# One expert block moved from behind a retrieval head to behind the last scores, and the weight split moved inside GpSimd's decoding

## The chip, the cores and the metric

The kernel runs on one core of one Trainium2 chip. The metric is the time of one execution on the device, in microseconds (us), lower is better. Its engines are TensorE (PE; its weight loads are PEld), VectorE (DVE), ScalarE (ACT), GpSimd (POOL) and the queue of SyncE (SP), which issues most DMAs.

## What is computed

One layer of a decoder with 1024 tokens of width 1024: a first half that mixes tokens, then a PEER layer: eight heads each pick 16 of 128 x 128 experts by product keys. The change touches the retrieval of this second half and the products with expert rows that are made ahead beside it.

```python
q = (hf @ w_query).reshape(n, PEER_HEADS, 2, PEER_HALF)
scores = jnp.einsum('nhpd,hpkd->nhpk', q, sub_keys).astype(jnp.float32)
s_top, i_top = lax.top_k(scores, PEER_TOPK)
cand_s = (s_top[:, :, 0, :, None] + s_top[:, :, 1, None, :]).reshape(n, PEER_HEADS, PEER_TOPK * PEER_TOPK)
cand_i = (i_top[:, :, 0, :, None] * N_KEYS + i_top[:, :, 1, None, :]).reshape(n, PEER_HEADS, PEER_TOPK * PEER_TOPK)
best_s, best_pos = lax.top_k(cand_s, PEER_TOPK)
idx = jnp.take_along_axis(cand_i, best_pos, axis=-1)
gates = jax.nn.softmax(best_s, axis=-1).astype(h.dtype)
...
u = jnp.take(expert_u, idx_blk, axis=0)
act = jax.nn.gelu(jnp.einsum('thkd,td->thk', u, h_blk))
```

## The kernel before

Products in float32 are made as three passes over upper and lower halves: an operand is split into an upper part (`hi`) and the rest (`lo`). The function `retrieve` is one block of programs, one for each engine; they meet only at its end and are otherwise ordered by semaphores and by the order of each program.

**Heads.** For each head d of 8, TensorE makes four units of queries (L195, 24 matmuls of 128x512 each) and two groups of scores (L1511) with the keys. ScalarE copies queries (L1581) and scores (L1590) out of the banks. VectorE searches the scores for the best 16 of either half (`search`, L1643 to L1655), adds them and ranks the sums (`combine`, L1672 on; it raises `ranked`). GpSimd then decodes the places (`decode`, L1459 to L1477), subtracts them from a row of numbers (L1482), ScalarE makes one-hots of the difference (`one_hot`, L1575 and L1577), GpSimd multiplies these by the indices (L1488), and VectorE sums them up (`conclude`, L1713, L1715, L1718), for head h - 1 behind the ranking of head h. ScalarE also takes the exponentials of a ranked head (`exponentials`, L1564 and L1567), at the beginning of the chunk two heads later.

**Query weights** come in a ring of two slots. SP loads one (L159) when the slot's raw part has been split, ScalarE makes the upper half (`split_hi`, L164), GpSimd the lower half (`split_lo`, L170, 128x2048). TensorE starts head d when both are there. In GpSimd's program the split for head h + 2 stands ahead of `decode(h)`, so that of head h + 3 stands directly behind the multiplications of head h.

**Blocks ahead.** Beside the heads TensorE already makes products with blocks of 128 expert rows (class `Ahead`), which the dense part of the expert stage reads later. A block n is: `turn` (L1343, eight transposes of the rows loaded by L1328), ScalarE's `upper` copy (L1369), `leave` (L1351, TensorE subtracts the upper part in the bank), ScalarE's `lower` copy (L1376), `hide` (L1361, two times 24 matmuls of 128x320), ScalarE's `gelu` (L1383) of either half, and SP's `store` (L1332). `turn` waits for both GELUs of the block before. There are 21 blocks: nine in `retrieve`, twelve in the scatter stage behind it. Of the nine, six stand in heads 2 to 7 (`IN_HEADS`, `FIRST` = 2), three behind the last scores (`IN_TAIL`).

**Tail.** Behind the last scores each of the three blocks also has two halves of rows (`rows_by_token`, L1544) that TensorE turns back to rows of tokens and ScalarE copies to `h_rows` (L1629), six halves in all. ScalarE has `exponentials(6)` ahead of the tail's blocks, `one_hot(6)` in the first of them ahead of its GELUs, and `exponentials(7)` in the last ahead of its GELUs. VectorE searches and ranks head 7 meanwhile, decodes it itself, concludes heads 6 and 7 and normalises the gates; the last step waits for `exponentials(7)`. SP waits at the end for the last store to land.

Of the kernel before, what the change touches and what calls it, by code (L numbers as in the profile page):

```python
# [37 lines left out]
PH, TOPK, NKEYS = 8, 16, 128  # L38
# [258 lines left out]
class Middle:  # L297


    U = 8  # L300
# [985 lines left out]
class Ahead:  # L1286


    FIRST, IN_HEADS, IN_TAIL = 2, 6, 3
    HEADS = IN_HEADS + IN_TAIL  # L1290
    EVERY = NKEYS // 8
    EXTRA = 5
# [101 lines left out]
def retrieve(nc, core, t, ring, begin, w_query, h, pick_i, pick_j, gate, ahead, h_rows):  # L1394
# [26 lines left out]
    last_ab, last_iota = core.at("rt_last_ab", 82, [P, 2, HB, 2], BF16), core.at("rt_last_iota", 83, [P, TOPK, 2], BF16)  # L1421
    last_place, last_eighth, last_less = (core.at(f"rt_last_part{k}", 84 + k / 2, [P, TT * TOPK]) for k in range(3))
    h_turned, h_copied = (core.sem(f"rt_{n}", lasting=RETRIEVE) for n in ("h_turned", "h_copied"))
    NPAIR, U = PH // 2, 4
    JOBS, FIRST_JOB = ahead.IN_HEADS, ahead.FIRST

    with nc.Block() as block:

        @block.sync
        def _(sp):  # L1430
            def query_weights(d):
                ring.load(sp, d % 2, d // 2, [(0, w_query[0, :, d * CW:(d + 1) * CW])])

            query_weights(2)
            query_weights(3)
            ahead.load(sp, 0, 0)
            ahead.load(sp, 1, 1)
            query_weights(4)
            query_weights(5)
            for n in range(ahead.HEADS):  # L1440
                if n + 2 < ahead.HEADS:
                    ahead.load(sp, n + 2, n % 2)
                for half in range(2):
                    ahead.store(sp, n, half)
                if n + 6 < PH:
                    query_weights(n + 6)
            for half in range(2):
                sp.wait_ge(ahead.stored[half], ahead.HEADS * 16)

        @block.gpsimd  # L1450
        def _(pool):
            pool.sem_inc(ring.lo_done[1], 1)
            ring.split_lo(nc.gpsimd, pool, 1, 0, U)

            def decode(h, s):

                pl, (a, b) = place[:].rearrange("p t k -> p (t k)"), (ab[s][:, 0, :], ab[s][:, 1, :])
                pool.wait_ge(ranked, h + 1)
                nc.gpsimd.tensor_copy(place_f[:], pl)  # L1459
                nc.gpsimd.tensor_copy(top_f[s][:], top_i[s])  # L1460
                pool.drain().then_inc(placed, 1)
                nc.gpsimd.tensor_scalar(eighth[:], place_f[:], 0.125, -0.4375, ALU.mult, ALU.add)
                nc.gpsimd.tensor_scalar(less[:], place_f[:], float(TOPK), 8.0, ALU.is_lt, ALU.mult)
                pool.drain()
                nc.gpsimd.tensor_scalar(eighth[:], eighth[:], ROUND, -ROUND, ALU.add, ALU.add)
                nc.gpsimd.tensor_tensor(less[:], less[:], place_f[:], ALU.add)
                pool.drain()
                nc.gpsimd.tensor_scalar(eighth[:], eighth[:], -1.0, 0.0, ALU.add, ALU.max)
                nc.gpsimd.tensor_scalar(place_f[:], place_f[:], -72.0, 0.0, ALU.add, ALU.max)
                pool.drain()  # L1470
                nc.gpsimd.tensor_tensor(a, place_f[:], eighth[:], ALU.add)
                pool.drain()
                nc.gpsimd.tensor_scalar(place_f[:], a, -8.0, -8.0, ALU.mult, ALU.add)
                pool.drain()
                nc.gpsimd.tensor_tensor(b, place_f[:], less[:], ALU.add)
                pool.drain()
                nc.gpsimd.tensor_scalar(b, b, 0.0, None, ALU.max)  # L1477
                pool.drain()
                if h >= 1:
                    pool.wait_ge(concluded, h)  # L1480
                for p in range(2):
                    nc.gpsimd.tensor_tensor(hot[p], ab[s][:, p, :].unsqueeze(2).to_broadcast([P, TT * TOPK, TOPK]),  # L1482
                                            t.iota16[:].unsqueeze(1).to_broadcast([P, TT * TOPK, TOPK]),
                                            ALU.subtract).then_inc(apart, 1)
                for p in range(2):
                    hot4 = hot[p].rearrange("p (t k) a -> p t k a", t=TT)
                    pool.wait_ge(hot_done, h * 2 + (p + 1))
                    nc.gpsimd.tensor_tensor(hot4, hot4, top_f[s][:, :, p, :].unsqueeze(2).to_broadcast([P, TT, TOPK, TOPK]),  # L1488
                                            ALU.mult).then_inc(picked, 1)

            for i in range(NPAIR - 1):
                for s in range(2):
                    ring.split_lo(nc.gpsimd, pool, s, i + 1, i * 2 * U + (s + 2) * U)
                    decode(i * 2 + s, s)
            decode(PH - 2, 0)
            core.clear_early(pool)

        @block.tensor
        def _(pe):
            ahead.prime_tensor(pe)  # L1500

            def units(d, half, j):
                ring.channels_unit(nc, pe, core.bank[j % 2], d % 2, j % 2, h, half, d * U + j)

            def scores(h, half):
                pe.wait_ge(q_copied, h * U + 2 * half + 2)
                for m in range(2 * half, 2 * half + 2):
                    pe.wait_ge(sc_copied, 4 + h * U + m - 1)
                    for k in range(4):
                        tt, p = 2 * m + k // 2, k % 2  # L1510
                        last = nc.tensor.matmul(core.bank[4 + m % 2][:, k * P:(k + 1) * P], q[:, p, tt * P:(tt + 1) * P],  # L1511
                                                sk_t[:, 2 * h + p, :], start=True, stop=True)
                    last.then_inc(scored, 1)

            for d in range(PH):
                n = d - FIRST_JOB
                job = 0 <= n < JOBS
                if d:
                    ring.ready(pe, d % 2, d // 2)
                    units(d, 0, 0)  # L1520
                if job:
                    ahead.turn(pe, n, n % 2, n // 2)
                if d:
                    units(d, 0, 1)
                scores(d, 0)
                if job:
                    ahead.leave(pe, n, n % 2)
                units(d, 1, 2)
                if job:
                    ahead.hide(pe, n, n % 2, 0)  # L1530
                units(d, 1, 3)
                if job:
                    ahead.hide(pe, n, n % 2, 1)
                scores(d, 1)
            def rows_by_token(n):

                tile, k0 = DENSE // P + n // 2, (n % 2) * 4
                if n < 2:
                    pe.wait_ge(sc_copied, 4 * PH + n + 3)
                else:  # L1540
                    pe.wait_ge(h_copied, n - 1)
                for k in range(4):
                    for a, part in enumerate((h.lo, h.hi)):
                        last = nc.tensor.matmul(core.bank[4 + n % 2][:, k * P:(k + 1) * P],  # L1544
                                                part[:, k0 + k, tile * P:(tile + 1) * P].bitcast(F32), t.ident[:], start=a == 0, stop=a == 1)
                last.then_inc(h_turned, 1)

            for k in range(ahead.IN_TAIL):
                n = JOBS + k
                ahead.turn(pe, n, n % 2, n // 2)  # L1550
                rows_by_token(2 * k)
                ahead.leave(pe, n, n % 2)
                rows_by_token(2 * k + 1)
                for half in range(2):
                    ahead.hide(pe, n, n % 2, half)

        @block.scalar
        def _(act):
# [12 lines left out]
            def one_hot(h):  # L1571

                for p in range(2):
                    act.wait_ge(apart, h * 2 + (p + 1))
                    nc.scalar.activation(hot[p], hot[p], ACT.Square)  # L1575
                    act.drain()
                    nc.scalar.activation(hot[p], hot[p], ACT.Relu, scale=-1.0, bias=1.0).then_inc(hot_done, 1)  # L1577
# [45 lines left out]
            for k in range(ahead.IN_TAIL):  # L1623
                job = JOBS + k
                ahead.upper(act, job, job % 2)
                ahead.lower(act, job, job % 2)
                for n in range(2 * k, 2 * k + 2):
                    act.wait_ge(h_turned, n + 1)
                    nc.scalar.activation(h_rows[:, n // 2, (n % 2) * HALF:(n % 2 + 1) * HALF], core.bank[4 + n % 2], ACT.Copy).then_inc(h_copied, 1)  # L1629
                if k == 0:  # L1630
                    one_hot(PH - 2)
                if k == ahead.IN_TAIL - 1:
                    exponentials(PH - 1)
                for half in range(2):
                    ahead.gelu(act, job, half)
# [1035 lines left out]
```

## Time and profile before

| | |
|---|---|
| runs | 3179.38, 3179.74, 3186.13 us; median 3179.74 |
| profiled execution | 3184.67 us, its span 3182.9 us |
| mean granted clock of TensorE | 0.983 of 2.4 GHz |
| busy share of the span | PE 95%, DVE 77%, POOL 38%, ACT 35% |
| retrieval | 846 to 1151 us of the span |
| scatter stage behind it | 1151 to about 1347 us |
| expert stage | from about 1347 us to the end |

A line of a timeline has the start and the duration of an instruction, or of several merged (x8), its engine, line, operation and operands, and in brackets the idle time of the engine before it and what ended that. Merged rows of matmuls overlap at their ends by some tenths of a microsecond, so the start of the next row tells better when a group was done.

### The profile page before, as it was taken

How to read it: one execution, taken by the hardware profiler on the slowest of the kernel's cores; microseconds unless marked ns; L12 is line 12 of the kernel's file. 1: busy time of each engine (PE TensorE's matmuls, PEld its weight loads, DVE VectorE, ACT ScalarE, POOL GpSimd, SP SyncE). 2: the span in 40 equal slices, each digit the busy share in tenths (PEclk: the TensorE clock that was granted, in tenths of full speed). 3: DMA queues.
4: the chain of work that ended last, by engine and by line, in shares of the span. 5: the costliest groups of instructions: out<-in, count | busy, mean ns of one | idle time of the engine just before them, and what ended most of it. 6: DMA issues, size and time to landing. Idle time of an engine off the chain costs nothing.

```text
span 3182.9 us, 52635 instructions
## 1 busy us (share of the span) xinstructions
PE 3032.1 (95%) x18287; PEld 2699.4 (85%) x18287; DVE 2456.8 (77%) x4956; ACT 1107.2 (35%) x2044; POOL 1206.6 (38%) x966
## 2 busy tenths in 40 slices
PE   6999999999999989969999999999999999999995
PEld 4998888779888878868898898889889888888884
DVE  5455333465589989978888888988888898999987
ACT  4222666503355655522232222222222222222222
POOL 0001000010158710035545545555555555555551
PEclk9999999999999999979999999999999999999998
DMA  6436333234211128899889889988988899999995
GB/s 239 147 123 195 108 107 106 84 119 140 95 37 56 33 74 251 264 349 329 315 319 336 323 311 328 326 300 326 336 325 317 319 334 329 346 339 347 335 333 208
DMA packets 353546, 764.41 MB, mean 240 GB/s; under 512 B 21020, under 2 KB 178808, under 8 KB 353408
## 3 DMA queue, kind: packets, MB, share of 16 engines
q0 software_dynamic: 115712, 419.48, 36.2%
q1 hardware_dynamic: 236640, 338.93, 31.5%
q10 hardware_dynamic: 1056, 4.19, 0.3%
q8 instruction: 82, 1.34, 0.2%
q14 instruction: 56, 0.46, 0.0%
HBM read 688.49 MB, written 74.03 MB: 240 GB/s over the span
## 4 chain that ended last, share of the span: by engine, by line
PE 50%; DVE 5%; issue 3%; DMA 3%; DVEq 2%; ACT 1%; POOL 0%; POOLq 0%; ACTq 0%; SPq 0%
PE psum L2174 22%; PE psum L2181 21%; PE psum L1361 3%; PE psum L2166 2%; PE psum L1876 2%; DVE ex_u_row L2381 2%; DMA ex_un<-in_expert_u 1%; DVE acc L2394 1%; DMA ex_v_row<-in_expert_v,ex_row 1%; DVEq L2391 1%; DVEq L2384 1%; DVE acc L2434 0%; DVE h_lo L2371 0%; PE psum L1343 0%; DVE fi_xs L2566 0%
## 5 line engine op out<-in xcount | busy, mean ns | idle before, releaser
L2122 POOL DMA_INDIRECT ex_u_row<-in_expert_u,ex_row x384 | 446.8, 1164 | 858.2 <-DVE ex_dot L2381 565.4
L2122 POOL DMA_INDIRECT ex_v_row<-in_expert_v,ex_row x384 | 518.4, 1350 | 150.5 <-issue 110.7
L2394 DVE SCALAR_TENSOR_TENSOR acc<-ex_v_row,ex_coef,acc 128x1024 f32<-128x1024 f32 x384 | 492.9, 1284 | 45.0 <-DMA ex_v_row<-in_expert_v,ex_row 17.9
L2381 DVE CUSTOM_DVE_ANT_0 ex_u_row<-ex_u_row,h_rows 128x1024 f32<-128x1024 f32 x384 | 467.3, 1217 | 1.9 <-DMA ex_u_row<-in_expert_u,ex_row 1.6
L2181 PE MATMUL psum<-ex_v_hi,ex_c_lo 128*128 128x512 f32 x1260 | 359.9, 408 | 22.7 <-DVE h_lo L2371 14.2
L2181 PE MATMUL psum<-ex_v_lo,ex_c_hi 128*128 128x512 f32 x1260 | 339.2, 391 | 0.0
L2181 PE MATMUL psum<-ex_v_hi,ex_c_hi 128*128 128x512 f32 x1260 | 338.6, 391 | 0.0
L2174 PE MATMUL psum<-h_hi,h_lo 128*128 128x320 f32 x1712 | 288.2, 311 | 19.2 <-DVE h_lo L2371 19.2
L2174 PE MATMUL psum<-h_lo,h_hi 128*128 128x320 f32 x1712 | 288.3, 311 | 0.0
L2174 PE MATMUL psum<-h_hi 128*128 128x320 f32 x1712 | 286.4, 310 | 0.0
L2174 PEld LDWEIGHTS psum<-h_hi,h_lo 128*128 128x128 f32 x1712 | 263.8, 189 | 24.8 <-DVE h_lo L2371 15.6
L2181 PEld LDWEIGHTS psum<-ex_v_lo,ex_c_hi 128*128 128x128 f32 x1260 | 237.1, 188 | 51.4
L2181 PEld LDWEIGHTS psum<-ex_v_hi,ex_c_hi 128*128 128x128 f32 x1260 | 237.0, 188 | 51.2
L2181 PEld LDWEIGHTS psum<-ex_v_hi,ex_c_lo 128*128 128x128 f32 x1260 | 222.2, 189 | 64.5 <-DVE h_lo L2371 20.1
L2174 PEld LDWEIGHTS psum<-h_lo,h_hi 128*128 128x128 f32 x1712 | 262.3, 189 | 0.0
L2174 PEld LDWEIGHTS psum<-h_hi 128*128 128x128 f32 x1712 | 260.4, 188 | 0.0
L2263 ACT ACTIVATE h_hi<-psum 128x512 fp32r<-128x512 f32 x214 | 127.1, 597 | 311.7 <-PE psum L2166 311.4
L2289 ACT ACTIVATE ex_c_hi<-ex_g 128x320 fp32r<-128x320 f32 x190 | 86.2, 470 | 410.3 <-DVE ex_g L2414 250.2
L2269 ACT ACTIVATE ex_v_hi<-ex_vn 128x2048 fp32r<-128x2048 f32 x63 | 120.2, 1909 | 262.7 <-PE psum L2181 262.7
L2376 DVE TENSOR_TENSOR ex_v_lo<-ex_vn,ex_v_hi 128x2048 fp32r<-128x2048 f32 x63 | 144.4, 2293 | 44.2 <-ACT ex_v_hi L2269 43.9
L2434 DVE TENSOR_TENSOR acc<-psum,acc 128x512 f32<-128x512 f32 x189 | 129.4, 685 | 59.1 <-PE psum L2181 59.1
L2371 DVE TENSOR_TENSOR h_lo<-psum,h_hi 128x512 fp32r<-128x512 f32 x214 | 142.8, 685 | 14.0 <-ACT h_hi L2263 11.6
(347 smaller groups left out, 5447.7 us busy)
## 6 DMA issues: line engine op xcount, KB each, us to landing
ex_vn<-in_expert_v SPq DMA_DIRECT2D x64, 1024.0 KB, 6.3
ex_un<-in_expert_u SPq DMA_DIRECT2D x43, 1024.0 KB, 8.7
w_dram<-sc_w SPq DMA_DIRECT2D x10, 4096.0 KB, 15.0
ex_w<-w_dram SPq DMA_DIRECT2D x64, 640.0 KB, 9.5
gm_wm<-in_w_mod SPq DMA_DIRECT2D x16, 1024.0 KB, 5.1
pj_raw<-in_w_in SPq DMA_DIRECT2D x11, 1024.0 KB, 8.4
ex_un<-in_expert_u SPq DMA_DIRECT2D x21, 512.0 KB, 7.0
qk_dram<-pj_staged_r POOLq DMA_DIRECT2D x32, 256.0 KB, 3.1
```

What stands on the lines that cost most here:

```text
L1361: last = self.nc.tensor.matmul(self.hide_bank[half][:, 0:HD], lhsT, rhs, start=i == 0, stop=i == len(ops) - 1)
L2122: nc.gpsimd.indirect_dma_start(to[:], None, all_rows, bass.IndirectOffsetOnAxis(row[s][:, col:col + 1], 0)).then_inc(done, 16)
L2174: last = nc.tensor.matmul(core.bank[bank][:, 0:HD], lhsT, rhs, start=m == 0, stop=m == len(ops) - 1)
L2181: last = nc.tensor.matmul(out, lhsT, rhs, start=m == 0 and not kept, stop=m == len(ops) - 1, skip_group_check=kept)
L2263: nc.scalar.activation(ut(h.hi, q // 2, (q % 2) * 4, 4), core.bank[banks[q]].rearrange("p (k n) -> p k n", k=4), ACT.Copy).then_inc(u_hi, 1)
L2269: nc.scalar.activation(vh.hi[:], vn[:], ACT.Copy).then_inc(v_hi, 1)
L2289: nc.scalar.activation(c_hi_at[c_set(j)][e][:, half * HD:(half + 1) * HD], x(j, n, first)[:], ACT.Copy).then_inc(c_hi, 1)
L2371: nc.vector.tensor_tensor(ut(h.lo, q // 2, (q % 2) * 4, 4), core.bank[bank].rearrange("p (k n) -> p k n", k=4), ut(h.hi, q // 2, (q % 2) * ...
L2376: nc.vector.tensor_tensor(vh.lo[:], vn[:], vh.hi[:].bitcast(F32), ALU.subtract).then_inc(v_lo, 1)
L2381: nc.vector.tensor_tensor_reduce(out=u_row[k % 3][:], in0=u_row[k % 3][:], in1=h_rows[:, k % 3, :], scale=1.0, scalar=0.0, op0=ALU.mult, o ...
L2394: nc.vector.scalar_tensor_tensor(out=to, in0=v_row[k % 3][:], scalar=coef[:, k:k + 1], in1=to, op0=ALU.mult, op1=ALU.add).then_inc(row_use ...
L2434: nc.vector.tensor_tensor(to, core.bank[banks[n]], to, ALU.add).then_inc(added, 1)
```

## The change

`IN_HEADS` goes from 6 to 5 and `IN_TAIL` from 3 to 4. The five blocks stand in heads 2 to 6, head 7 has none, and four stand behind the last scores. The first of these has no halves of rows beside it; the other three have two each, so that the six halves stand where three blocks are again. `one_hot(6)` stays in the first block of the tail, `exponentials(7)` in the last.

In GpSimd's program the split for head 2 stays ahead of `decode(0)`. Those for heads 3 to 7 go into `decode(h)`, between the subtraction and the multiplications, each with the same waits as before.

```diff
-    FIRST, IN_HEADS, IN_TAIL = 2, 6, 3
+    FIRST, IN_HEADS, IN_TAIL = 2, 5, 4
...
@@ retrieve, decode on GpSimd
                                             ALU.subtract).then_inc(apart, 1)
+                if h + 3 < PH:
+                    ring.split_lo(nc.gpsimd, pool, (h + 3) % 2, (h + 3) // 2, (h + 3) * U)
                 for p in range(2):
                     hot4 = hot[p].rearrange("p (t k) a -> p t k a", t=TT)
                     pool.wait_ge(hot_done, h * 2 + (p + 1))
...
-            for i in range(NPAIR - 1):
-                for s in range(2):
-                    ring.split_lo(nc.gpsimd, pool, s, i + 1, i * 2 * U + (s + 2) * U)
-                    decode(i * 2 + s, s)
-            decode(PH - 2, 0)
+            ring.split_lo(nc.gpsimd, pool, 0, 1, 2 * U)
+            for d in range(PH - 1):
+                decode(d, d % 2)
...
@@ retrieve, tail on TensorE
                 ahead.turn(pe, n, n % 2, n // 2)
-                rows_by_token(2 * k)
+                if k:
+                    rows_by_token(2 * k - 2)
                 ahead.leave(pe, n, n % 2)
-                rows_by_token(2 * k + 1)
+                if k:
+                    rows_by_token(2 * k - 1)
...
@@ retrieve, tail on ScalarE
-                for n in range(2 * k, 2 * k + 2):
+                for n in range(2 * max(k, 1) - 2, 2 * k):
```

## Rows read from the trace of the kernel before

**Rows 1.** Windows: length; busy of PE, PEld, DVE, ACT, POOL; clock; DMA share; GB/s.

```profile
967.00:1002.00 35.00, 34.29 (x188) 29.95 (x188) 33.92 (x202) 21.95 (x40) 27.45 (x19) 1.00 0.17 59
...
1122.00:1126.00 4.00, 3.82 (x22) 3.85 (x23) 3.71 (x26) 1.21 (x3) 2.48 (x1) 0.63 0.23 86
1126.00:1136.00 10.00, 9.95 (x70) 9.61 (x69) 9.28 (x56) 2.62 (x6) 0.00 (x0) 0.98 0.04 16
...
1160.00:1164.00 4.00, 3.39 (x12) 2.35 (x13) 4.00 (x4) 1.79 (x3) 0.00 (x0) 0.50 0.41 121
```

**Rows 2.** Timeline of TensorE, scores: heads 0 and 1, 6 and 7.

```profile
863.95 2.05 PE L1511 MATMUL psum<-rt_sk_t,rt_q 128*128 128x128 f32 x16 [0.71 <-ACTq L1582]
...
891.32 2.05 PE L1511 MATMUL psum<-rt_sk_t,rt_q 128*128 128x128 f32 x16 [0.71 <-ACTq L1582]
...
1044.91 2.05 PE L1511 MATMUL psum<-rt_sk_t,rt_q 128*128 128x128 f32 x16 [0.71 <-ACTq L1582]
...
1079.67 2.05 PE L1511 MATMUL psum<-rt_sk_t,rt_q 128*128 128x128 f32 x16 [0.71 <-ACTq L1582]
...
1099.97 1.94 PE L1511 MATMUL psum<-rt_sk_t,rt_q 128*128 128x128 f32 x16
```

**Rows 3.** Timeline of GpSimd, heads 4 to 6.

```profile
1052.43 8.23 POOL L1488 TENSOR_TENSOR rt_hots<-rt_hots,rt_top_f 128x2048 bf16<-128x2048 bf16 x2 [6.02 <-ACT rt_hots L1577]
1060.61 4.65 POOL L170 TENSOR_TENSOR rt_w_lo<-rt_raw,rt_w_hi 128x2048 fp32r<-128x2048 f32 x1
...
1097.31 0.29 POOL L1459 CAST rt_part<-rt_place 128x128 f32<-128x128 uint32 x1 [1.86 <-DVEq L1684]
...
1105.60 7.32 POOL L1482 TENSOR_TENSOR rt_hots<-rt_ab,iota 128x2048 bf16<-128x2048 f32 x2
```

**Rows 4.** Timeline of VectorE: conclusions, searches, the last step.

```profile
922.98 4.34 DVE L1713 TENSOR_TENSOR rt_hots<-rt_hots 128x2048 bf16<-128x2048 bf16 x1
...
1062.58 3.77 DVE L1713 TENSOR_TENSOR rt_hots<-rt_hots 128x2048 bf16<-128x2048 bf16 x1
...
1068.61 0.29 DVE L1643 MAX8 rt_top<-rt_sc 128x8 f32<-128x128 f32 x1
...
1097.32 1.35 DVE L1713 TENSOR_TENSOR rt_hots<-rt_hots 128x2048 bf16<-128x2048 bf16 x1
...
1102.60 0.28 DVE L1643 MAX8 rt_top<-rt_sc 128x8 f32<-128x128 f32 x1 [1.76 <-issue]
...
1146.81 1.23 DVE L1753 TENSOR_TENSOR pick<-pick,rt_einv 128x1024 f32<-128x1024 f32 x1
```

**Rows 5.** Line L1713: durations in ns (least, median, most), first and last start.

```profile
L1713 DVE TENSOR_TENSOR rt_hots<-rt_hots x7: 1226/3661/4342, 923.0 to 1139.0; 128x2048 bf16<-128x2048 bf16 x7
```

**Rows 6.** Timeline of ScalarE: scores of head 6, then the tail.

```profile
1067.20 0.60 ACT L1590 ACTIVATE rt_sc<-psum 128x512 f32<-128x512 f32 x1 [0.30 <-PE psum L1511]
...
1104.51 0.22 ACT L1564 ACTIVATE rt_lowest<-rt_best 128x8 f32<-128x8 f32 x1
1104.79 1.28 ACT L1567 ACT_TABLE_LOAD   x1
...
1108.43 1.05 ACT L1369 ACTIVATE ah_hi<-psum 128x512 fp32r<-128x512 f32 x2
...
1112.34 1.90 ACT L1575 ACTIVATE rt_hots<-rt_hots 128x2048 bf16<-128x2048 bf16 x1
...
1118.10 1.91 ACT L1577 ACTIVATE rt_hots<-rt_hots 128x2048 bf16<-128x2048 bf16 x1
```

**Rows 7.** Timeline of TensorE: second and third block of the tail, next stage.

```profile
1122.18 1.16 PE L1343 MATMUL psum<-ident,ah_un_rt 128*128 128x128 f32 x8 [3.34 <-issue]
...
1136.53 1.06 PE L1343 MATMUL psum<-ident,ah_un_rt 128*128 128x128 f32 x8 [0.57 <-issue]
...
1147.33 1.33 PE L1361 MATMUL psum<-h_hi,ah_hi 128*128 128x320 f32 x8
1151.43 2.81 PE L1815 MATMUL psum<-ident,pick 128*128 128x128 f32 x24 [2.76 <-PEq L1427]
```

More of the change, by code:

```diff
@@ L1423, in retrieve @@
     h_turned, h_copied = (core.sem(f"rt_{n}", lasting=RETRIEVE) for n in ("h_turned", "h_copied"))
-    NPAIR, U = PH // 2, 4
+    U = 4
     JOBS, FIRST_JOB = ahead.IN_HEADS, ahead.FIRST
```

## The prediction

> **What bounds the kernel now.** The edit lies in one stage, the retrieval (846 to 1151 us of the span), so I leave the shares of the whole run and read that stage engine by engine, in the timeline. In its heads the reader is to look for the engine that is never idle. It is TensorE: a head with a block ahead takes 34.76 us, and in every such head TensorE waits once, 0.71 us, for ScalarE's copy of the queries [rows 1, 2]. GpSimd waits 6.0 us in each head for ScalarE's one-hot passes [rows 3]. VectorE looks full in the same window [rows 1], but part of that is no work: its first halving of the one-hots (L1713) takes 1.23 us where GpSimd is still. In the five heads in which it starts while GpSimd runs the weight split of L170 it takes 3.64 to 4.34 us, and ends about 1.2 us after that split [rows 3 to 5]. So VectorE has at least 2.4 us of slack in a head, and in the last head it shows in the open: with no split beside it L1713 takes 1.35 us, and then VectorE waits 1.76 us for scores [rows 4].
>
> Behind the last scores there are two chains. VectorE searches the last head and ends at 1148.0 (1146.81 + 1.23) [rows 4]. TensorE does three blocks and six halves of rows, ends at 1148.66, and what follows it (the GELU, its store, the landing, the meeting of all engines) opens the next stage at 1151.43 [rows 7]. TensorE's chain is the later one, by 0.6 us of its own and 2.8 us of what follows. This tail is not dense: a block can turn only when ScalarE has written the GELUs of the block before, and for the second of the three that came behind the one-hot passes of head 6, with TensorE idle for 3.34 us.
>
> **The split of query weights (first edit).** Nothing is added or removed; five splits of 4.63 us (heads 3 to 7) go from behind GpSimd's multiplications to ahead of them. Their slot is GpSimd's 6.0 us wait: the subtraction ends at 1046.4, the split would end at 1051.1, and the multiplication may start at 1052.4 [rows 3]. Cost 0. If that cover were gone, up to 4.6 us per head would lie between the one-hot passes and VectorE's halving. The loads of later weights are issued sooner on SP's queue; nobody waits for them now. VectorE's halving then meets only GpSimd's short casts, so the row with 1.35 us is the one to take, and the five stretched ones, some 2.5 us each, give back about 12.4 us. What is late next is the scores, and they come from TensorE: in the present run search 6 starts at 1068.61 and its scores were copied at 1067.80 [rows 4, 6]. So VectorE can gain 0.76 us before it waits again, and the rest of the 12.4 us becomes waiting.
>
> The Trainium skill, page "SBUF — State Buffer", section "Who interferes with whom", says that a VectorE instruction with two SBUF inputs and a GpSimd instruction that reads SBUF exclude each other, and that VectorE instructions with one SBUF input, as its searches are, go untouched. The trace agrees on both. Read by that rule alone the edit would be worth 12.4 us; read by the idle time ahead of the searches it is worth 0.76 us.
>
> **Five blocks in the heads (second edit), head 7.** Its block goes. From the second scores of head 0 to those of head 1, which has no block and two waits of 0.71 us, are 27.37 us; with a block a head takes 7.39 more [rows 2]. The last scores end at 1094.4, not 1101.8. What is that worth? VectorE can take them only when it has finished head 6: search 6 starts at 1067.85, its ranking ends 0.76 us earlier than now, at 1096.5, and conclusion 5 ends at 1100.1. So search 7 starts 2.5 us earlier than 1102.60. VectorE's chain gains 2.5 us, and it was not the later one.
>
> **The tail, four blocks.** First block (number 5), from 1094.4. ScalarE's program has head 6's exponentials, which need its ranking, ahead of its copies, so ScalarE stands until 1096.5. Before, this ranking was 7 us old when ScalarE got there (1104.51) [rows 6]. Exponentials take 2.6 us (3.92 less a table load of 1.28, which in the rows follows a GELU; if it stays, it hides in the next wait), then come upper and lower copies, and TensorE's products run from 1102 to about 1109. No rows stand beside the waits of this block: they are moved to the blocks behind it. Then ScalarE's order is one-hot, GELU. GpSimd starts to decode head 6 at 1096.55, takes 8.29 us to the subtraction and 3.67 us for its first half: 1108.5 [rows 3]. The two one-hots take 7.67 us, to 1116.2; from their end to the next turn are 2.17 us, for a table load and the GELUs [rows 6, 7]. The second block turns at 1118.4, against 1122.18 now: only 3.7 us earlier, though the last scores are 7.4 us earlier; TensorE idles about 9 us before it.
>
> From there go three blocks with two halves of rows each, where there are two now. The one behind the gap takes 14.35 us from turn to turn (1122.18 to 1136.53); its first 4 us ran at a mean granted clock of 0.63 (mostly 1.2 GHz), for which it pays about 1.6 us [rows 1, 7]. The next takes 12.13 us to the end of its products and 0.58 for GELU and handover, 12.71; the last 12.13. Sum: 1118.44 + 14.35 + 12.71 + 12.13 = 1157.63, against 1148.66: **+9.0 us.** The last exponentials stand beside the last products as now; VectorE normalises until about 1157, ahead of the store. The later stages start at the same meeting and hold the same twelve blocks, so they are shifted whole: 0.
>
> Against the profiled execution (3184.67 us, its span 3182.9) this is 3193.7. That execution is 4.9 us above the median; on the median, 3179.7 + 9.0 = **3188.7 us**. What no row shows is the clock behind 9 us of idling instead of 3.3. From below, the block pays nothing for it, -1.6 us; from above, the 4 us run at 0.50, as those behind the 6.3 us gap ahead of the next stage did, +0.4 [rows 1]. I take the present price, of the nearest kind of work. With 1 us either way for handovers, and 2 us above because no gap in the rows is so long: 3186.1 to 3192.1 for this case.
>
> **Rivals.** *VectorE sets the pace of the heads.* Then all of the 12.4 us is real: head 6's ranking comes at 1084.9 instead of 1097.3, the 63.9 us from it to the next stage stay, and that opens at 1148.8: -2.6 us, 3177.1. It decides if TensorE waits for VectorE anywhere in the heads. For it: VectorE is busy 97% of the window in rows 1; the skill's rule above is its mechanism. Against: TensorE has one wait per head, on ScalarE's copy. 7%. *GpSimd sets the pace*: five heads shorter by 4.63 us, ranking at 1074.1: -13.4 us, 3166.3. Against stand its own 6 us of waiting. 4%.
>
> *The first block of the tail is not held by the one-hots.* If its GELU came right behind its products, the second turn would come at 1109.8, and the same 39.2 us from there end at 1149.0, against 1148.66: +0.3, 3180.0, no change. Against: the order of ScalarE's program, and the present run's turn at 1122.18, directly behind the GELUs. 7%.
>
> *The clock stays low.* If TensorE runs the whole second block at 1.2 GHz, its remaining 9.5 us double: +18.5, 3198.2. For it: behind both gaps in rows 1 the clock was low; against: 4 us later its mean was 0.98 [rows 1]. 8%. The skill's page "TensorE: Matmul & The Clock Gate", section "HAM oscillation", warns of idle gaps between stretches of matmuls; the second edit makes such a gap longer. By the trace a gap costs 1.6 us, and the present run has it too.
>
> **How the numbers follow.** My case has 74%. A measurement of this kernel can tell about 0.2%, 6.4 us, from no change; the lower end of my case and the scatter of the runs (3179.38 to 3186.13) reach it: 0.62 slower, 0.12 same. With the rivals: slower 0.70; same 0.12 + 0.05 + 0.07 = 0.24; faster 0.04 + 0.02 = 0.06. The range takes in my case, the rival without change and the one with the low clock: 3178.5 to 3198.5; the two of the pace, and an odd run, are left out.
>
> **What would show it.** Heads 2 to 6 keep 34.76 us, L1713 falls to about 1.35 us, and the searches wait for scores about 2 us per head. GpSimd's wait at L1488 falls by about 1 us only, since it starts decoding sooner. The last scores end near 1094.4. TensorE then has two gaps, about 5 us ahead of the first subtraction and about 9 us ahead of the second turn (near 1118), and ends near 1157.6; the next stage opens near 1160.4. I am wrong if the heads shorten, if the second turn comes before 1112, or if a later stage gives the 9 us back.

## The result

| | us | ratio to before |
|---|---|---|
| before, first measurement | 3180.68 median of 5 runs (3179.38 to 3187.54) | |
| changed | 3196.23 median of 5 runs (3189.01 to 3197.46) | 1.0033, 95% interval 1.0022 to 1.0043 |
| profiled execution of the changed kernel | 3195.86, its span 3194.1 | |

The change makes the kernel slower by 0.33% (10.5 us of 3183). The difference of the two medians, 15.5 us, says more than it should: five runs of a kernel spread over 8 us, and in 28 runs beside the experiments the kernel before had a median of 3184.44. The ratio with its interval is what counts.

For the traces a measure is wanted that doesn't depend on how the earlier stages fell. The retrieval of the changed kernel's profile began 2.8 us earlier than that of before (its first scores of head 6 are at 1042.08, before at 1044.91 [rows 2]). The same shift already stands at the second scores of head 0 (861.11 against 863.95 [rows 2]), ahead of everything that the edits touch, so the change can't have caused it. So all times of the tail are counted here from these first scores of head 6. From there the next stage opened after 106.52 us before (1151.43 - 1044.91) and after 116.10 us now: **+9.6 us**.

The heads. Timeline of TensorE, scores of the changed kernel, beside [rows 2]:

```profile
1007.32 2.05 PE L1511 MATMUL psum<-rt_sk_t,rt_q 128*128 128x128 f32 x16 [0.71 <-ACTq L1584]
...
1042.08 2.05 PE L1511 MATMUL psum<-rt_sk_t,rt_q 128*128 128x128 f32 x16 [0.71 <-ACTq L1584]
...
1075.95 2.05 PE L1511 MATMUL psum<-rt_sk_t,rt_q 128*128 128x128 f32 x16 [0.71 <-ACTq L1584]
...
1089.63 2.05 PE L1511 MATMUL psum<-rt_sk_t,rt_q 128*128 128x128 f32 x16 [0.71 <-ACTq L1584]
```

From 1007.32 to 1042.08 are 34.76 us, as before. The last scores begin 47.55 us after the first of head 6, before 55.06 (1099.97 - 1044.91), and the wait of 0.71 us now stands ahead of them.

The moved split. Timeline of GpSimd (the split, then the multiplications of head 4), then of VectorE, conclusion and search of head 6, beside [rows 3, 4]:

```profile
1039.92 4.56 POOL L170 TENSOR_TENSOR rt_w_lo<-rt_raw,rt_w_hi 128x2048 fp32r<-128x2048 f32 x1
1049.61 8.25 POOL L1490 TENSOR_TENSOR rt_hots<-rt_hots,rt_top_f 128x2048 bf16<-128x2048 bf16 x2 [5.12 <-ACT rt_hots L1579]
1058.94 0.29 POOL L1459 CAST rt_part<-rt_place 128x128 f32<-128x128 uint32 x1 [1.09 <-DVEq L1686]
```

```profile
1058.96 1.35 DVE L1715 TENSOR_TENSOR rt_hots<-rt_hots 128x2048 bf16<-128x2048 bf16 x1
1065.02 0.28 DVE L1645 MAX8 rt_top<-rt_sc 128x8 f32<-128x128 f32 x1 [2.54 <-issue]
```

The split is done 5.1 us before GpSimd may go on, the halving (now L1715) takes 1.35 us, and VectorE then waits 2.54 us for scores that it did not have to wait for before (2.30 to 2.55 us in the five heads that had a stretched halving).

The tail. Timeline of TensorE, first products and the turns of the second to fourth block, the last products and the next stage, beside [rows 7]:

```profile
1096.93 1.27 PE L1351 MATMUL psum<-ah_hi,minus 128*128 128x512 f32 x2 [4.37 <-ACT ah_hi L1369]
...
1115.57 1.94 PE L1343 MATMUL psum<-ident,ah_un_rt 128*128 128x128 f32 x8 [7.40 <-issue]
...
1130.56 1.07 PE L1343 MATMUL psum<-ident,ah_un_rt 128*128 128x128 f32 x8 [0.57 <-issue]
...
1143.28 1.06 PE L1343 MATMUL psum<-ident,ah_un_rt 128*128 128x128 f32 x8 [0.57 <-issue]
...
1154.08 1.34 PE L1361 MATMUL psum<-h_hi,ah_hi 128*128 128x320 f32 x8
1158.18 4.32 PE L1817 MATMUL psum<-ident,pick 128*128 128x128 f32 x24 [2.76 <-PEq L1427]
```

TensorE waits 4.37 us for ScalarE's upper copy and 7.40 us ahead of the second turn. ScalarE at the same time, beside [rows 6]: it waits for the ranking, then for GpSimd's subtraction (its one-hots are now L1577 and L1579).

```profile
1093.67 0.21 ACT L1566 ACTIVATE rt_lowest<-rt_best 128x8 f32<-128x8 f32 x1 [1.35 <-DVEq L1686]
...
1105.72 1.91 ACT L1577 ACTIVATE rt_hots<-rt_hots 128x2048 bf16<-128x2048 bf16 x1 [6.87 <-POOL rt_hots L1482]
...
1111.48 1.91 ACT L1579 ACTIVATE rt_hots<-rt_hots 128x2048 bf16<-128x2048 bf16 x1
1113.41 1.28 ACT L1383 ACT_TABLE_LOAD   x1
1114.70 0.77 ACT L1383 ACTIVATE ah_g_rt<-psum 128x320 f32<-128x320 f32 x2
```

The GELUs end at 1115.47 (1114.70 + 0.77), the turn begins at 1115.57. VectorE is not the later chain; its last step waited 12.6 us for `exponentials(7)`:

```profile
1152.93 0.55 DVE L1752 RECIPROCAL rt_einv<-rt_esum 128x64 f32<-128x64 f32 x1 [12.60 <-ACT pick L1569]
```

### The profile page after: what moved, and what is told of

It reads as the page before. It is cut to its first block, busy times and chain, and to the rows that moved or that the text cites. A ratio compares the mean times of both kernels' runs of the same rounds, so it can differ in the third digit from the quotient of the medians.

```text
span 3194.1 us, 52633 instructions
## 1 busy us (share of the span) xinstructions
PE 3034.0 (95%) x18287; PEld 2699.4 (85%) x18287; DVE 2444.5 (77%) x4956; ACT 1105.1 (35%) x2042; POOL 1203.2 (38%) x966
## 4 chain that ended last, share of the span: by engine, by line
PE 50%; DVE 5%; issue 3%; DMA 2%; DVEq 2%; ACT 1%; POOL 0%; POOLq 0%; ACTq 0%; SPq 0%
PE psum L2176 22%; PE psum L2183 21%; PE psum L1361 3%; PE psum L2168 2%; PE psum L1878 2%; DVE ex_u_row L2383 2%; DMA ex_un<-in_expert_u 1%; DVE acc L2396 1%; DVEq L2393 1%; DMA ex_v_row<-in_expert_v,ex_row 1%; DVEq L2386 1%; DVE acc L2436 0%; DVE h_lo L2373 0%; PE psum L1343 0%; DVE fi_xs L2568 0%
## 6 DMA issues: line engine op xcount, KB each, us to landing
w_dram<-sc_w SPq DMA_DIRECT2D x10, 4096.0 KB, 14.9
```

## The experiments

Each is timed against the kernel before on the same chip. The table puts them side by side; the times of the tail are counted from the first scores of head 6, "first turn" is that of the next stage. The traces are of one execution each. Nine lie within 2 us of the median of their kernel; that of e8_three is the fastest of its 11 runs (3178.15 us, median 3184.17), so its trace may flatter it.

| kernel | second turn | next stage opens | first turn there | ratio to before (95%) |
|---|---|---|---|---|
| before | 77.3 | 106.5 | 115.6 | 1 |
| changed | 73.5 | 116.1 | 126.7 | 1.0033 (1.0022 to 1.0043) |
| e1_blocks_only | 74.3 | 117.4 | 128.2 | 1.0031 (1.0018 to 1.0043) |
| e2_split_only | 77.3 | 106.5 | 116.7 | 1.0000 (0.9991 to 1.0009) |
| e3_onehot_later | 66.5 | 109.7 | 118.9 | 1.0013 (1.0004 to 1.0022) |
| e4_rows_first | 73.5 | 114.2 | 123.4 | 1.0026 (1.0015 to 1.0036) |
| e5_both | 65.2 | 107.7 | 118.2 | 1.0006 (0.9997 to 1.0015) |
| e6_before_onehot_later | 74.5 | 108.4 | 119.2 | 1.0013 (1.0004 to 1.0023) |
| e7_exp_later | 73.5 | 116.0 | 126.4 | 1.0033 (1.0021 to 1.0046) |
| e8_three | 62.1 | 101.9 | 112.5 | 0.9996 (0.9987 to 1.0005) |

### The two edits apart

**e1_blocks_only**: five and four blocks, the split where it was before.

```diff
-                if h + 3 < PH:
-                    ring.split_lo(nc.gpsimd, pool, (h + 3) % 2, (h + 3) // 2, (h + 3) * U)
...
-            ring.split_lo(nc.gpsimd, pool, 0, 1, 2 * U)
-            for d in range(PH - 1):
-                decode(d, d % 2)
+            for i in range(NPAIR - 1):
+                for s in range(2):
+                    ring.split_lo(nc.gpsimd, pool, s, i + 1, i * 2 * U + (s + 2) * U)
+                    decode(i * 2 + s, s)
+            decode(PH - 2, 0)
```

> The block is moved, the split stays behind GpSimd's multiplications. Measure: from the first scores of head 6 to the opening of the next stage, 106.5 us in the kernel before, 116.1 in the changed one. My theory (the whole loss is the tail's): 116.9, since only the 0.8 us that head 6's ranking gained are given back; L1713 again 3.6 to 4.3 us in five heads; ratio to before 1.003. Rival (the split inside the decoding costs a part of the loss): 113 or less.

Measured: 117.4 us and 1.0031. The whole loss is there without the split's move. The halvings are stretched again:

```profile
L1715 DVE TENSOR_TENSOR rt_hots<-rt_hots x7: 1225/3664/4365, 921.3 to 1135.7; 128x2048 bf16<-128x2048 bf16 x7
```

Of the 1.3 us more than in the changed kernel, 0.8 are in the second turn (74.3 against 73.5), as the later ranking had to give; the other 0.5 are in the block behind it, 15.5 against 15.0 us from turn to turn.

**e2_split_only**: the kernel before with the split inside the decoding, the same lines the other way round.

> The split is moved, the blocks stay six and three. My theory (TensorE sets the pace of the heads): the heads keep 34.76 us, L1713 falls to about 1.35 us, the searches wait about 2 us more per head, and from the first scores of head 6 to the next stage are 106.5 us as before; ratio 1.000. Rival (VectorE sets the pace): five heads shorter by about 2.5 us, 12 us faster, ratio 0.996. Second rival (the split is not covered by the wait): heads longer by up to 4.6 us.

Measured: 106.5 us and 1.0000. Timeline of VectorE, head 6:

```profile
1061.86 1.35 DVE L1713 TENSOR_TENSOR rt_hots<-rt_hots 128x2048 bf16<-128x2048 bf16 x1
...
1067.92 0.28 DVE L1643 MAX8 rt_top<-rt_sc 128x8 f32<-128x128 f32 x1 [2.53 <-issue]
```

Five halvings gave back some 2.4 us each, and VectorE waits 2.53 us instead: the rival in which VectorE sets the pace is gone (it wanted 0.996). The split inside the decoding costs nothing either.

### What holds the second turn

**e3_onehot_later**: the changed kernel, head 6's one-hots in the second block of the tail.

```diff
-                if k == 0:
+                if k == 1:
                     one_hot(PH - 2)
```

> The changed kernel with head 6's one-hots one block later in ScalarE's tail. My theory (the second turn is held by these one-hots): it comes about 8 us earlier, directly behind the first block's products, the third turn about 15 us after it, and from the first scores of head 6 to the next stage are 107.6 us instead of 116.1; ratio to before about 1.0005. Rival (the loss is the fourth block's own work on TensorE, or the clock): 116, ratio 1.003.

Measured: 109.7 us, 1.0013. The second turn comes 7.0 us earlier, 0.57 us behind the first block's products:

```profile
1111.23 1.07 PE L1343 MATMUL psum<-ident,ah_un_rt 128*128 128x128 f32 x8 [0.57 <-issue]
...
1125.28 1.25 PE L1343 MATMUL psum<-ident,ah_un_rt 128*128 128x128 f32 x8 [1.91 <-issue]
...
1139.62 1.06 PE L1343 MATMUL psum<-ident,ah_un_rt 128*128 128x128 f32 x8 [0.57 <-issue]
```

So the hold was the one-hots: 6.4 of the 9.6 us go with it, though TensorE has the same work. Of the 2.1 us by which I missed, the second turn has 1.5 (at 66.5, where my sum had 65; under the first products, from 1098 to 1106, the granted clock was 0.59 and then 0.56) and the third block 1.6 (14.34 us against 12.7 for one at full clock, behind a gap of 1.91 us); a shorter second block (14.05, not 15.1) gives 1 back. The other 3.2 of the 9.6 us stay; the runs on the rows and on the first gap below are about them.

**e7_exp_later**: the changed kernel, head 6's exponentials behind the copies of the first block.

```diff
-            exponentials(PH - 2)
             for k in range(ahead.IN_TAIL):
...
                 ahead.lower(act, job, job % 2)
+                if k == 0:
+                    exponentials(PH - 2)
```

> The changed kernel with head 6's exponentials behind the copies of the tail's first block, so that ScalarE no longer stands for the ranking with that block's copies behind it. My theory: TensorE's first gap (4.4 us) nearly closes and the first block's products end 3 to 4 us earlier, but the second turn keeps its time (73.5 us from the first scores of head 6), since GpSimd's subtraction and the one-hots are on the path; 116.1 us to the next stage, ratio 1.003. Rival (the first gap is part of the loss): 112 to 113.

Measured: 116.0 us, 1.0033. The first gap shrinks by 4.1 us, from 4.37 to 0.30, and the second grows by 6.3, from 7.40 to 13.73: it takes back those 4.1 us and also the 2.3 us by which the first block's products are shorter (from the first subtraction to the beginning of the second gap 9.0 us, in the changed kernel 11.2):

```profile
1095.75 0.99 PE L1351 MATMUL psum<-ah_hi,minus 128*128 128x512 f32 x2 [0.30 <-ACT ah_hi L1369]
...
1118.47 1.94 PE L1343 MATMUL psum<-ident,ah_un_rt 128*128 128x128 f32 x8 [13.73 <-issue]
```

The turn itself stays at 73.5. The first of the two gaps is free as long as the second one is held.

### Where the rows stand

**e4_rows_first**: the changed kernel, halves of rows 0 and 1 in the first block, none in the third (the last two have to stay in the last block, since their tile shares memory with its expert rows).

```diff
-                if k:
-                    rows_by_token(2 * k - 2)
+                if k != 2:
+                    rows_by_token(2 * min(k, 2))
                 ahead.leave(pe, n, n % 2)
-                if k:
-                    rows_by_token(2 * k - 1)
+                if k != 2:
+                    rows_by_token(2 * min(k, 2) + 1)
...
-                for n in range(2 * max(k, 1) - 2, 2 * k):
+                for n in () if k == 2 else range(2 * min(k, 2), 2 * min(k, 2) + 2):
```

> The changed kernel with the first two halves of rows in the first block of the tail and none in the third; the one-hots stay in the first. My theory: the rows lie in the idle time of TensorE, the second turn keeps its time, the third block is 3.4 us shorter: 112.7 us from the first scores of head 6 to the next stage (116.1 in the changed kernel), ratio to before 1.002. Rival (the work counts wherever it stands): 116.1.

Measured: 114.2 us, 1.0026; the interval overlaps that of the changed kernel, so the trace has to decide. The second turn kept its time (73.5), the work lay in the gap, and 1.9 of the expected 3.4 us came out. A part of the rest is here, in the block without rows:

```profile
1133.86 0.98 PE L1351 MATMUL psum<-ah_hi,minus 128*128 128x512 f32 x2 [0.25 <-ACT ah_hi L1369]
1135.53 1.44 PE L1361 MATMUL psum<-h_hi,ah_lo 128*128 128x320 f32 x8 [0.69 <-ACT ah_lo L1376]
```

The rows had been the cover for ScalarE's two copies. With them TensorE doesn't wait inside a block; without them it takes 10.86 us from turn to turn (9.3 was expected, 12.7 with rows). The two waits are 0.9 us of the 1.6 that it takes beyond the 9.3; the other 0.6 are not accounted for.

**e5_both**: the edits of e3_onehot_later and e4_rows_first together.

> As the one before, and the first two halves of rows stand in the first block of the tail, none in the third. My theory: the rows fill the gap ahead of the first subtraction in part; second turn about 2 us later than without, third block 9.3 us instead of 12.7, so 106.0 us from the first scores of head 6 to the next stage, ratio to before 0.9998. Rival (the work on TensorE counts, wherever it stands): 107.6, no gain from moving rows.

Measured: 107.7 us, 1.0006. In the sense of the rival it is 107.6, but for another reason than the rival's: the third block took 13.56 us, for the same two waits and a clock that was low for some 7 us of it (from about 1125.5 to 1132.3), where the same block ran 10.86 us at full clock in the two other kernels that have it. Windows of this kernel (length; busy of PE, PEld, DVE, ACT, POOL; clock; DMA share; GB/s):

```profile
1122.00:1126.00 4.00, 2.05 (x10) 1.23 (x10) 3.93 (x35) 3.14 (x7) 4.00 (x2) 0.93 0.22 82
1126.00:1130.00 4.00, 3.73 (x14) 3.73 (x15) 3.58 (x26) 0.22 (x1) 1.03 (x1) 0.50 0.01 2
```

**e8_three**: all three moves of the tail.

> The changed kernel with all three moves in the tail: exponentials behind the first block's copies, head 6's one-hots in the second block, the first two halves of rows in the first block. My theory: with the one-hots out of the first block the first gap does count, so the second turn comes 3.4 us earlier than with the other two moves (61.8 us after the first scores of head 6, there 65.2), and the next stage opens at 104.4 us against 106.5 in the kernel before; ratio to before 0.9993 to 1.0000. Rival (the hold moves on to GpSimd's subtraction or the clock takes it back): 107 to 108, ratio 1.0006.

Measured: the second turn at 62.1 as expected, the next stage at 101.9, 4.6 us earlier than in the kernel before, and 0.9996 in time, which can't be told from 1. With the hold gone the first gap does count (62.1 against 65.2): what e7_exp_later showed to be free costs 3 us here. The 2.5 us beyond my figure are the third block, which in this execution, the fastest of the eleven, kept full clock behind the same gap as in e5_both (10.86 us, there 13.56):

```profile
1118.00:1122.00 4.00, 2.30 (x11) 1.48 (x12) 3.79 (x31) 2.84 (x7) 4.00 (x2) 1.00 0.23 84
1122.00:1126.00 4.00, 4.00 (x29) 4.00 (x29) 3.85 (x33) 0.43 (x1) 0.50 (x1) 1.00 0.01 2
```

So a block behind the heads, with these three moves beside it, costs nothing that the times can tell; whether it beats the kernel before is not shown.

### The same move in the kernel before

**e6_before_onehot_later**: six and three blocks, the split behind the multiplications, `one_hot(6)` in the second block of the tail (the line of e3_onehot_later).

> The kernel before with head 6's one-hots one block later. My theory (they hold the second turn there too, by 3 us, and would then hold the third): second turn 3 us earlier, third 1.6 us earlier, 104.9 us from the first scores of head 6 to the next stage against 106.5; ratio 0.9995, not to be told from 1 in the times. Rival (no hold in that kernel): 106.5.

Measured: 108.4 us, 1.0013: slower, where I expected a gain of 1.6 us in the trace. On TensorE the expectation held, and more: the second turn comes 2.8 us earlier (74.5), the third 3.1 (1133.63 - 1045.07 = 88.6, before 91.6), and its last products are done at 1145.8, 100.7 us after the first scores of head 6, 3.0 us earlier than before (1148.66). Then it idles 7.68 us ahead of the next stage. VectorE had become the later chain:

```profile
1131.49 1.90 DVE L1690 TENSOR_SCALAR rt_shifted_place<-rt_place 128x128 uint32<-128x128 uint32 x1
1133.31 4.14 DVE L1691 CAST rt_last_part<-rt_place 128x128 f32<-128x128 uint32 x1
...
1151.85 1.23 DVE L1753 TENSOR_TENSOR pick<-pick,rt_einv 128x1024 f32<-128x1024 f32 x1
```

In the kernel before these two took 0.23 and 0.22 us:

```profile
1131.30 0.23 DVE L1690 TENSOR_SCALAR rt_shifted_place<-rt_place 128x128 uint32<-128x128 uint32 x1
1131.44 0.22 DVE L1691 CAST rt_last_part<-rt_place 128x128 f32<-128x128 uint32 x1
```

In e6_before_onehot_later they meet GpSimd's multiplications, which the later one-hots have moved over them:

```profile
1129.18 8.19 POOL L1488 TENSOR_TENSOR rt_hots<-rt_hots,rt_top_f 128x2048 bf16<-128x2048 bf16 x2 [16.07 <-ACT rt_hots L1577]
```

The first ends near the end of the first multiplication (1133.3), the second with the second (1137.4). That is 5.6 us more on VectorE; less the 0.65 us that its last two steps waited for `exponentials(7)` before, it is the 4.9 us by which they end later (1153.1 - 1045.1 = 108.0 against 103.1). That it is the collision was read from these ends; no run took it away alone. The other traces bear it out: in all nine the multiplications are over before the two begin or within 0.3 us of it, and the two take 0.23 to 0.30 and 0.21 to 0.22 us. In e3_onehot_later, with the same later one-hots, head 7 comes earlier and head 6's multiplications end at 1129.00, 0.2 us after the first of the two began:

```profile
1120.82 8.18 POOL L1490 TENSOR_TENSOR rt_hots<-rt_hots,rt_top_f 128x2048 bf16<-128x2048 bf16 x2 [8.81 <-ACT rt_hots L1579]
```

```profile
1128.79 0.30 DVE L1692 TENSOR_SCALAR rt_shifted_place<-rt_place 128x128 uint32<-128x128 uint32 x1
1129.01 0.21 DVE L1693 CAST rt_last_part<-rt_place 128x128 f32<-128x128 uint32 x1
```

## Why the prediction was right

Forecast 3188.7 on a median of 3179.7, +9.0 us, in a range of 3178.5 to 3198.5; measured +10.5 by the ratio (7.0 to 13.7 by its interval). So the difference was forecast well. The absolute time was not: the measured median, 3196.23, lies above the 3186.1 to 3192.1 of my own case, and is within the range because that also takes in the rival with the low clock. The base had most of that miss: I took the median of three runs, 3179.7, where 28 later runs of the same kernel have 3184.4, and 3184.4 + 9.0 would have been 3193.4. Point by point:

- *TensorE sets the pace of the heads*: right, 34.76 us in either kernel, and e2_split_only excludes both rivals of the pace. (In the rival of VectorE, the 63.9 us from the ranking of head 6 to the next stage are those of my forecast, 1160.4 - 1096.5, not of the kernel before, where they are 54.1.)
- *The split's slot costs nothing, and the 12.4 us turn into waiting*: right, L1713 fell to 1.35 us, and the waits ahead of the searches are 2.3 to 2.55 us a head. GpSimd's wait fell by 0.9 us to 5.1, as said.
- *A head without a block is 7.39 us shorter*: right to 0.1: the last scores begin 7.5 us earlier, and the merged row's end, with the wait ahead of it, fits 1094.4 after the shift of 2.8 us. It was worth taking this from two heads of the trace that differ in just this, not from a sum of durations.
- *The second turn*: forecast 73.5 us after the first scores of head 6 (1118.44 - 1044.91; the terms as written give 1118.35), measured 73.5. The chain was the named one: ranking, GpSimd's decoding and subtraction, one-hots, GELU; e3_onehot_later takes it out, e7_exp_later shows that the other gap is not on it. The gap itself was 7.4 us, not 9: the first products ran at a granted clock of 0.50 from 1098 to 1102 and took longer, which the gap swallowed. That the turn hits the forecast to 0.1 us is therefore no credit to the times that I gave for the products; it hangs on the other chain.
- *Three blocks from there*: forecast 14.35, 12.71 and 12.13, measured 14.99, 12.72 and 12.13. Only the first was mis-sized, by 0.6: the price of the clock. I took it from a gap of 3.3 us; behind 7.4 us it was low for longer. The other traces agree: behind gaps of 3.34 us this block took 14.35 and 14.28 us (before, e2_split_only), behind gaps of 6.2 to 13.7 us 14.9 to 15.5 (the changed kernel, e1_blocks_only, e4_rows_first, e7_exp_later).

```profile
1110.00:1115.50 5.50, 0.00 (x0) 0.00 (x0) 5.42 (x37) 5.37 (x5) 5.50 (x2) 0.51 0.00 0
1115.50:1119.50 4.00, 3.93 (x19) 3.96 (x20) 3.71 (x23) 1.20 (x2) 2.32 (x1) 0.50 0.47 125
1119.50:1130.00 10.50, 10.49 (x73) 10.14 (x72) 9.78 (x67) 2.61 (x5) 0.00 (x0) 0.96 0.14 52
```

  In these windows of the changed kernel the clock is 0.51 to 0.50 from before the turn until 4 us behind it, where [rows 1] had a mean of 0.63 over the 4 us. The rival in which it stays low through the block is excluded.
- *The later stages are shifted whole, 0*: not shown to be wrong. From the opening to the first turn of the next stage are 10.6 us, before 9.1. The 24 transposes at the opening took 4.32 us, before 2.81, behind an equal gap of 2.76 us: at a clock of 0.67 over 5 us there, 1.00 before. That is 1.5 us, but the change need not have caused it. In e2_split_only the tail is that of the kernel before to 0.1 us, and the transposes took 4.06 us all the same:

```profile
1151.45 4.06 PE L1815 MATMUL psum<-ident,pick 128*128 128x128 f32 x24 [2.77 <-PEq L1427]
```

  From that first turn to the end of the span the changed kernel took 2.9 us more; across the ten traces this remainder lies between 2020.9 and 2025.3 us, 2022.4 for the kernel before, so that difference is not explained by the change and I leave it open.

The opening comes 9.6 us later, and with the 1.5 us of the transposes 11.1; either lies within the 7.0 to 13.7 us of the interval around the measured 10.5. The two profiled spans differ by 11.2 us (3194.1 - 3182.9) because the 2.8 us by which the changed kernel's retrieval began earlier and the open 2.9 us behind it cancel, which is luck.

## What to carry to other kernels

Work moved from a busy place to an idle one gains only what the moved work lets start earlier; here 7.4 us of TensorE bought 2.4 us for VectorE, which was not the later chain, and the work met a program order on a third engine (GELUs behind one-hots) that held everything behind it. A second such order (copies behind a ranking) cost nothing as long as the first held (e7_exp_later), and 3 us when it didn't (e5_both against e8_three). Before such a move, walk through the order of each engine's program at the new place and date every wait from its own chain. And where two gaps stand in a row, only the one whose end is held from outside counts: closing the other moves it, until the hold is gone.

Where a helper engine's work can slide, look at what it slides over: the same one-line edit gained 6.4 us in one kernel (e3_onehot_later) and lost 1.9 in the other (e6_before_onehot_later). There TensorE had only 3.0 us to gain, and GpSimd's multiplications landed on two small VectorE instructions.

## What the runs showed of the hardware that I had not expected

- Two VectorE instructions on 128 x 128 elements, 0.23 and 0.22 us alone, took 1.90 and 4.14 us beside GpSimd's multiplications of 128x2048. They have one tensor input each, and the prediction said of such instructions that they go untouched. That was too wide. The Trainium skill, page "SBUF — State Buffer", section "Who interferes with whom", excepts VectorE's two-port modes from it, and names casts and `tensor_scalar` among those that can take the pair of ports that VectorE shares with GpSimd, in these modes. The trace agrees by its ends (1133.4 and 1137.4, those of the two multiplications); which mode the two ran in no trace shows. The ranking's searches of 128x80, just ahead of them and beside the same multiplications, kept 0.23 us.
- Equal idle gaps of TensorE do not have equal prices. Behind a gap of 1.91 us the third block of the tail ran at full clock in two kernels (e6_before_onehot_later, e8_three, granted clock 1.00) and in part at 1.2 GHz in two (e3_onehot_later, 0.59 over the first 4 us; e5_both, 0.50 over 4 us), a difference of 1.6 to 2.7 us. At the opening of the next stage the same 24 transposes took 2.81 us in three traces (before, e3_onehot_later, e4_rows_first) and 4.06 to 4.48 us in the others, behind a gap of 2.76 us in all but e6_before_onehot_later (7.68). So a single trace carries some 3 us of this, and a claim smaller than that needs the same row in several kernels.
